# Every 512-column product of a float32r kernel issued as two of 256 columns

## The chip, the cores and the metric

The kernel runs on one core of a Trainium2 chip. The metric is the device time of one execution in microseconds (us). The kernel before takes 1372.56 us, the median of three runs.

## The reference

The program runs two model blocks over 256 tokens with 1024 features in float32. The first has two layers, each a root-mean-square norm, a mixer and a residual sum: an S5 state-space mixer, then block attention with eight heads. The second has two layers of feed-forward, hybrid mixer (a pooling branch and an HGRN2 branch), feed-forward, and a final norm. Nearly all of the arithmetic is products of the tokens with weight matrices. Cut to those:

```python
proj = h @ w_in                                   # S5: 1024 x 2048; attention: 1024 x 4096
y = y * jax.nn.sigmoid(y @ w_glu + b_glu)         # 1024 x 1024
out = y @ w_out                                   # 1024 x 1024, four times in all
def swiglu(x, w_gate, w_up, w_down):              # 1024 x 2816 twice, 2816 x 1024; four times
    return (jax.nn.silu(x @ w_gate) * (x @ w_up)) @ w_down
z = h @ w_in                                      # hybrid mixer: 1024 x 4608, twice
merged = g[:, :, 0] * (pool_out @ w_pool_proj) + g[:, :, 1] * (hgrn_out @ w_hgrn_proj)
return merged @ w_out
```

## The kernel before, in words

**Products in three parts.** A float32 product is made from three float32r products. Each operand is split in two float32r tiles, high and low: weights into WH and WL, tokens into RH and RL (R2H and R2L for a second set, HHI and HLO for the hidden rows of a feed-forward). `mm3` (line 414) issues high × high, high × low and low × high into the same place in PSUM. Each `matmul` brings its own load of the stationary operand, so TensorE's page row counts as many weight loads (PEld) as products (PE). In the profile's names, `P<-RH,WH` is a product that moves RH past stationary WH into PSUM bank P; the products of every helper stand under line 412.

**Two orientations.** Where the result is wanted with features on the partitions, the weights are stationary (128 columns) and the 256 tokens move: `linear` (425), `gate_up_columns` (806), `last_gate` (735), `pool_product` (896). These products have 256 moving columns and write half of a 512-column PSUM bank. Where tokens are wanted on the partitions, 128 tokens are stationary and 512 weight columns move, which fill a whole bank: `out_rows` (454, the four output projections; 32 threes each), `value_rows` (641, 16 threes in each of two mixers), `rows` (664, queries and keys 64 threes, values 32), `gate_up` (786, the first 256 hidden features of each of four feed-forwards, 16 threes each), `gate_rows` (910, 16 in each mixer) and `down` (835, 8 threes for each of 11 blocks of hidden features in four feed-forwards).

**Staging.** The weights come in 222 units of 1 MB through a ring of five slots. SyncE issues a unit's transfer into RAW when the unit that used the slot before is done (`unit_used`, raised by TensorE behind its last product with it). ScalarE copies it into WH (line 1005, `hi_split`), VectorE subtracts to get WL (line 1435, `lo_split`), and TensorE waits for `lo_split`. Each engine's order is written out by hand and the engines meet by semaphores alone.

**Order around the change.** A feed-forward (`ffn`, 848) has eleven blocks of 256 hidden features. The first is made by `gate_up` and turned by transposes; from the second on, `gate_up_columns` issues 96 products of 256 columns, followed by `down` of the block before with 24 products of 512. The last two blocks of `gate_up_columns` stand together, then the remaining 66 and six products of `down` end the block. At its end the residual sum, the norm on VectorE and ScalarE, the transposes (`turn_norm`, 439) and the split of the normed tokens into RH and RL (line 1447) lead into the next block; part of that is laid between products. In the mixers and in attention, short groups of other products (128 columns for the levels, scores and transposes) stand between groups of 24 to 240 long ones.

**The accumulation flag.** A product with `start` set clears the bank's marks of what was written, and a later product without it overwrites where nothing is marked and adds where something is. The kernel relies on this already where two halves of a bank are built in turn: in the first gate unit (line 632) only the first half's product has `start`.

Of the kernel before, what the change touches and what calls it, by code (L numbers as in the profile page):

```python
# [7 lines left out]
KT = DM // 128  # L8
# [96 lines left out]
def build(nc, A, out):  # L105
# [4 lines left out]
    with ctx:  # L110
        def sb(name, shape, dt=f32, c=ctx):
            return c.enter_context(nc.sbuf_tensor(name, shape, dt))


        c = ExitStack()
        RAW = sb("RAW", [128, NW, 2048], c=c)
        c.close()
        c = ExitStack()
# [5 lines left out]
        c = ExitStack()  # L124
# [16 lines left out]
        c = ExitStack()  # L141
        TMPD = sb("TMPD", [128, 2048], c=c)
        c.close()
        c = ExitStack()
# [4 lines left out]
        c = ExitStack()  # L149
# [3 lines left out]
        c = ExitStack()  # L153
# [15 lines left out]
        c = ExitStack()  # L169
# [5 lines left out]
        c = ExitStack()  # L175
# [9 lines left out]
        c = ExitStack()  # L185
# [12 lines left out]
        RH = sb("RH", [128, KT, T], f32r, c=outer)  # L198
        RL = sb("RL", [128, KT, T], f32r, c=outer)
# [3 lines left out]
        c = ExitStack()  # L203
# [20 lines left out]
        c = ExitStack()  # L224
        SG = sb("SG", [128, 2, T], c=c)
        HF = sb("HF", [128, 2, T], c=c)
        HHI = sb("HHI", [128, 3, 2, T], f32r, c=c)
        HLO = sb("HLO", [128, 3, 2, T], f32r, c=c)
        c.close()
        c = ExitStack()  # L230
# [17 lines left out]
        P = [PP[i // 2][:, (i % 2) * 512:(i % 2) * 512 + 512] for i in range(8)]  # L248
# [4 lines left out]
        def tok(a):  # L253
            return slice(a * 128, a * 128 + 128)
# [138 lines left out]
        def _(eng):  # L393
# [20 lines left out]
            def mm3(o, lh, ll, rh, rl, start, stop):  # L414

                mm(o, lh, rh, start=start, stop=False, skip_group_check=True)
                mm(o, lh, rl, start=False, stop=False, skip_group_check=True)
                return mm(o, ll, rh, start=False, stop=stop, skip_group_check=True)

            def weights(u, kt):  # L420

                wh = WH[:, slot_of(u), :].rearrange("p (k c) -> p k c", k=kt)
                return wh, WL[:, slot_of(u), :].rearrange("p (k c) -> p k c", k=kt)
# [30 lines left out]
            def out_rows(u0, i, xh, xl, ready="r_lo", between=None):  # L454


                for n in range(2):
                    for kh, a in ((0, 0), (0, 1), (1, 0), (1, 1)) if n == 0 else ((0, 0), (1, 0), (0, 1), (1, 1)):
                        if kh == 0:
                            free(2 * a + n)  # L460
                        eng.wait_ge(sem["lo_split"], parts_of(u0 + 2 * n + kh))
                        wh, wl = weights(u0 + 2 * n + kh, 4)
                        for k in range(4):
                            kk = 4 * kh + k
                            if n == 0 and a == 0 and k % 2 == 0:
                                eng.wait_ge(sem[ready], pe.next(ready))
                            last = mm3(P[2 * a + n][:, :], xh[:, kk, tok(a)], xl[:, kk, tok(a)],
                                       wh[:, k, :], wl[:, k, :], kk == 0, kk == KT - 1)
                            if n == 1 and a == 1 and kk == 5:
                                turn_norm(i, 0)  # L470
                        if a:
                            last.then_inc(sem["unit_used"], 1)
                        elif kh:
                            last.then_inc(sem["acc_done"], 1)
                        if kh:
                            holds(2 * a + n, "resid")
                        if between is not None and n == 0 and a == 0 and kh == 0:
                            between()
# [27 lines left out]
            for cb in range(1, 4):  # L506
# [6 lines left out]
                for ri in range(2):  # L513
                    for m in range(KT):
                        v = CX[:, ri, m, :]
                        last = nc.tensor.transpose(P[4 + ri * 2 + m // 4][:, (m % 4) * 128:(m % 4) * 128 + 128], v, IDENT)
# [106 lines left out]
            wh, wl = weights(U_GLU, KT)  # L623
# [17 lines left out]
            def value_rows(u0, i, banks):  # L641

                for n in range(len(banks)):
                    for a in range(2):
                        free(banks[n][a])
                        for kh in range(2):
                            u = u0 + 2 * n + kh
                            eng.wait_ge(sem["lo_split"], parts_of(u))
                            wh, wl = weights(u, 4)
                            if n == 0:  # L650
                                eng.wait_ge(sem["xn_lo"], 4 * i - 4 + 2 * a + kh + 1)
                            for k in range(4):
                                kk = 4 * kh + k
                                last = mm3(P[banks[n][a]][:, :], RH[:, kk, tok(a)], RL[:, kk, tok(a)],
                                           wh[:, k, :], wl[:, k, :], kk == 0, kk == KT - 1)
                                if n == 0 and a == 0 and kk == 5:
                                    turn_norm(i, 1)
                            if a:
                                last.then_inc(sem["unit_used"], 1)
                        if not a:  # L660
                            last.then_inc(sem["rows_done"], 1)
                        holds(banks[n][a], "bank_read_a")

            def rows(u, a, bank, part, read):


                if not part:
                    free(bank)
                eng.wait_ge(sem["lo_split"], parts_of(u + part))
                if u == U_QK:  # L670
                    eng.wait_ge(sem["xn_lo"], 4 * N_ATTN - 4 + 2 * a + part + 1)
                wh, wl = weights(u + part, 4)
                for k in range(4):
                    kk = 4 * part + k
                    last = mm3(P[bank][:, :], RH[:, kk, tok(a)], RL[:, kk, tok(a)], wh[:, k, :], wl[:, k, :], kk == 0, kk == KT - 1)
                    if u == U_QK and not a and kk == 5:
                        turn_norm(N_ATTN, 1)
                if a:
                    last.then_inc(sem["unit_used"], 1)
                elif part:  # L680
                    last.then_inc(sem["rows_done"], 1)
                if part:
                    holds(bank, read)
# [102 lines left out]
            def gate_up(u, a, j, i, mid=None):  # L786

                free(4 + a)
                for kh in range(2):
                    eng.wait_ge(sem["lo_split"], parts_of(u + kh))  # L790
                    if j == 0:
                        eng.wait_ge(sem["xn_lo"], 4 * i - 4 + 2 * a + kh + 1)
                    wh, wl = weights(u + kh, 4)
                    for k in range(4):
                        kk = 4 * kh + k
                        last = mm3(P[4 + a][:, :], RH[:, kk, tok(a)], RL[:, kk, tok(a)], wh[:, k, :], wl[:, k, :],
                                   kk == 0, kk == KT - 1)
                        if mid is not None and kk == 5:
                            mid()
                    if a:  # L800
                        last.then_inc(sem["unit_used"], 1)
                if not a:
                    last.then_inc(sem["gu_done"], 1)
                holds(4 + a, "h_made")
# [30 lines left out]
            def down(f, u, j, a, n):  # L835

                eng.wait_ge(sem["lo_split"], parts_of(u))
                eng.wait_ge(sem["h_lo"], 22 * f + 2 * j + (2 if j else a + 1))
                if j == 0:
                    free(2 * a + n)  # L840
                wh, wl = weights(u, 2)
                for k in range(2):
                    last = mm3(P[2 * a + n][:, :], HHI[:, j % 3, k, tok(a)], HLO[:, j % 3, k, tok(a)],
                               wh[:, k, n * 512:n * 512 + 512], wl[:, k, n * 512:n * 512 + 512],
                               j == 0 and k == 0, j == NF - 1 and k == 1)
                return last
# [63 lines left out]
            def gate_rows(u, a):  # L910


                free(a)
                for kh in range(2):
                    if not a:
                        eng.wait_ge(sem["lo_split"], parts_of(u + kh))
                    wh, wl = weights(u + kh, 4)
                    for k in range(4):
                        kk = 4 * kh + k
                        last = mm3(P[a][:, :], RH[:, kk, tok(a)], RL[:, kk, tok(a)], wh[:, k, :], wl[:, k, :], kk == 0, kk == KT - 1)  # L920
                    if a:
                        last.then_inc(sem["unit_used"], 1)
                if not a:
                    last.then_inc(sem["rows_done"], 1)
                holds(a, "bank_read_v")
# [1263 lines left out]
```

## Time and profile before

| what | value |
|---|---|
| median of three runs | 1372.56 us |
| the three runs | 1370.96, 1372.56, 1375.68 us |
| span of the profiled execution, first to last instruction | 1370.1 us |
| TensorE busy, products | 1346.6 us, 9502 products |
| VectorE busy | 868.0 us |
| ScalarE busy | 715.9 us |
| mean granted TensorE clock | 0.999 |
| weights and inputs read | 240.17 MB, 176 GB/s |

The profiled execution's own time is given as its span; the median of the runs is 2.5 us above it. "Busy" for TensorE is the union of overlapping durations: the end of a product is modelled, and a product starts well before the one ahead of it has ended. The distance between two products is read from their starts in the timeline, not from a duration. In the chain that ended last, a piece is a stretch of time on one engine, with the count of instructions in it.

### The profile page before, as it was taken

The numbers are of one execution on the slowest core, as the hardware profiler recorded it, in microseconds if no ns is written. First come the engines' busy times: TensorE is split into PE (matmuls) and PEld (weight loads), VectorE is DVE, ScalarE is ACT, GpSimd is POOL, SyncE is SP. The second block draws the span as 40 slices with busy tenths as digits, with TensorE's granted clock in tenths as the row PEclk, the third lists the DMA queues.
The fourth block names the chain that finished last, engine by engine and source line by source line (L and its number), as shares of the span: only waits on it lengthen the run. The fifth ranks groups of instructions, "written<-read, shape, count | busy, mean of one in ns | idle before, by whom it ended". The sixth has DMA issues, their size and how long they took to land.

```text
span 1370.1 us, 22005 instructions
## 1 busy us (share of the span) xinstructions
PE 1346.6 (98%) x9502; PEld 1244.3 (91%) x9502; DVE 868.0 (63%) x1012; ACT 715.9 (52%) x954; POOL 56.4 (4%) x68
## 2 busy tenths in 40 slices
PE   7998999999999999999999999999999999999998
PEld 6998879889999989998999998999989999899997
DVE  6999676766445567767655547544566857655553
ACT  5998566664444453375544445444454345544443
POOL 1003000000000004000000000000000400000000
PEclk9999999999999999999999999999999999999999
DMA  9106556455656465355555565665556436655552
GB/s 278 53 32 209 180 173 199 140 186 179 201 197 194 167 217 165 120 186 189 195 185 185 192 208 172 201 200 196 201 173 212 152 107 211 198 186 185 185 185 92
DMA packets 180387, 242.63 MB, mean 177 GB/s; under 512 B 7546, under 2 KB 144004, under 8 KB 180292
## 3 DMA queue, kind: packets, MB, share of 16 engines
q1 hardware_dynamic: 178260, 234.92, 52.4%
q0 software_dynamic: 1744, 6.10, 1.6%
q8 instruction: 75, 1.23, 0.4%
q10 hardware_dynamic: 288, 0.22, 0.1%
q14 instruction: 20, 0.16, 0.0%
HBM read 240.17 MB, written 1.05 MB: 176 GB/s over the span
## 4 chain that ended last, share of the span: by engine, by line
PE 96%; ACT 1%; DVE 1%; DMA 1%; issue 0%; DVEq 0%; ACTq 0%; POOLq 0%
PE P L412 94%; PE P L447 1%; DMA G<-in_norm_g 1%; ACT BT L1132 1%; DVE WL L1435 0%; DVE RL L1447 0%; PE P L690 0%; DVE X L1457 0%; ACT YG L1160 0%; PE P L720 0%; ACT Y L1021 0%; DVE YS L1471 0%; ACT RH L1031 0%; ACT WH L1005 0%; PE P L831 0%
## 5 line engine op out<-in xcount | busy, mean ns | idle before, releaser
L1435 DVE TENSOR_TENSOR WL<-RAW,WH 128x2048 fp32r<-128x2048 f32 (+1 forms) x211 | 480.6, 2285 | 304.6 <-ACT WH L1005 303.7
L412 PE MATMUL P<-RH,WH 128*128 128x256 f32 x1856 | 515.9, 278 | 4.0 <-DVE RL L1447 2.7
L412 PE MATMUL P<-RL,WH 128*128 128x256 f32 x1856 | 513.1, 276 | 0.0
L412 PE MATMUL P<-RH,WL 128*128 128x256 f32 x1856 | 513.0, 276 | 0.0
L1005 ACT ACTIVATE WH<-RAW 128x2048 fp32r<-128x2048 f32 x214 | 406.6, 1903 | 189.6 <-DMA RAW<-in_ffn_w_up 78.6
L412 PEld LDWEIGHTS P<-RH,WH 128*128 128x128 f32 x1856 | 348.7, 188 | 5.9 <-DVE RL L1447 2.3
L412 PEld LDWEIGHTS P<-RL,WH 128*128 128x128 f32 x1856 | 348.7, 188 | 1.5
L412 PEld LDWEIGHTS P<-RH,WL 128*128 128x128 f32 x1856 | 348.4, 188 | 0.0
L412 PE MATMUL P<-WH,HLO 128*128 128x512 f32 x352 | 138.7, 394 | 0.0
L412 PE MATMUL P<-WL,HHI 128*128 128x512 f32 x352 | 138.0, 392 | 0.0
L412 PE MATMUL P<-WH,HHI 128*128 128x512 f32 x352 | 136.9, 389 | 0.0
L1316 ACT ACTIVATE SG<-P 128x256 f32<-128x256 f32 x88 | 33.8, 384 | 177.6 <-PE P L412 177.5
L412 PE MATMUL P<-WH,RH 128*128 128x512 f32 x288 | 116.0, 403 | 1.7 <-DVE RL L1447 1.7
L412 PE MATMUL P<-WH,RL 128*128 128x512 f32 x288 | 113.4, 394 | 0.0
L412 PE MATMUL P<-WL,RH 128*128 128x512 f32 x288 | 112.7, 391 | 0.0
L412 PEld LDWEIGHTS P<-WL,HHI 128*128 128x128 f32 x352 | 66.1, 188 | 13.8
L412 PEld LDWEIGHTS P<-WH,HLO 128*128 128x128 f32 x352 | 66.2, 188 | 13.1
L412 PEld LDWEIGHTS P<-WH,HHI 128*128 128x128 f32 x352 | 66.1, 188 | 13.2
L412 PEld LDWEIGHTS P<-WH,RH 128*128 128x128 f32 x288 | 54.2, 188 | 14.1 <-issue 3.0
L412 PEld LDWEIGHTS P<-WH,RL 128*128 128x128 f32 x288 | 54.1, 188 | 11.9
L412 PEld LDWEIGHTS P<-WL,RH 128*128 128x128 f32 x288 | 54.2, 188 | 10.9
L1915 DVE TENSOR_TENSOR HF<-P,SG 128x256 f32<-128x256 f32 x88 | 37.0, 422 | 42.5 <-ACT SG L1316 41.9
(304 smaller groups left out, 1429.5 us busy)
## 6 DMA issues: line engine op xcount, KB each, us to landing
RAW<-in_ffn_w_gate SPq DMA_DIRECT2D x88, 512.0 KB, 4.2
RAW<-in_ffn_w_up SPq DMA_DIRECT2D x88, 512.0 KB, 5.3
RAW<-in_ffn_w_down SPq DMA_DIRECT2D x44, 1024.0 KB, 4.9
RAW<-in_w_in SPq DMA_DIRECT2D x36, 1024.0 KB, 5.1
RAW<-in_attn_w_in SPq DMA_DIRECT2D x16, 1024.0 KB, 5.4
RAW<-in_ssm_w_in SPq DMA_DIRECT2D x8, 1024.0 KB, 9.3
RAW<-in_w_out SPq DMA_DIRECT2D x8, 1024.0 KB, 5.1
RAW<-in_ssm_w_glu SPq DMA_DIRECT2D x4, 1024.0 KB, 6.6
```

Of the source, the lines that this page charges most:

```text
L412: return nc.tensor.matmul(*a, **k)
L447: last = nc.tensor.transpose(P[6 + n][:, k * 128:k * 128 + 128], y[:, a, c:c + 128], IDENT)
L1005: fn(WH[:, s, 0:width], RAW[:, s, 0:width], ACT.Copy).then_inc(sem["hi_split"], 1)
L1132: fn(BT[:, ri, j0:j0 + 4, :], P[4 + g % 4].rearrange("p (j s) -> p j s", j=4), ACT.Copy).then_inc(sem["bt_there"], 1)
L1316: fn(SG[:, a, :], P[4 + a][:, 0:T], ACT.Silu).then_inc(act.raised("gate_done"), 1)
L1435: V.tensor_tensor(WL[:, s, 0:width], RAW[:, s, 0:width], WH[:, s, 0:width].bitcast(f32), SUB).then_inc(sem["lo_split"], 1)
L1915: V.tensor_tensor(HF[:, a, :], P[4 + a][:, T:2 * T], SG[:, a, :], MUL).then_inc(dve.raised("h_made"), 1)
```

## The change

A helper `mm3w` issues what one `mm3` on 512 columns did as two `mm3` on 256 columns each: the three products for the first half of the bank, then the three for the second half. The stationary operands are the same in both halves and are loaded again. Only the first half's first product keeps `start`, since it clears the marks of the whole bank. All six places with 512 moving columns call it.

```diff
+            def mm3w(o, lh, ll, rh, rl, start, stop):
+
+
+                for i in range(2):
+                    c = slice(i * 256, i * 256 + 256)
+                    last = mm3(o[:, c], lh, ll, rh[:, c], rl[:, c], start and i == 0, stop)
+                return last
+
@@ out_rows
-                            last = mm3(P[2 * a + n][:, :], xh[:, kk, tok(a)], xl[:, kk, tok(a)],
+                            last = mm3w(P[2 * a + n][:, :], xh[:, kk, tok(a)], xl[:, kk, tok(a)],
                                        wh[:, k, :], wl[:, k, :], kk == 0, kk == KT - 1)
@@ down
-                    last = mm3(P[2 * a + n][:, :], HHI[:, j % 3, k, tok(a)], HLO[:, j % 3, k, tok(a)],
+                    last = mm3w(P[2 * a + n][:, :], HHI[:, j % 3, k, tok(a)], HLO[:, j % 3, k, tok(a)],
                                wh[:, k, n * 512:n * 512 + 512], wl[:, k, n * 512:n * 512 + 512],
                                j == 0 and k == 0, j == NF - 1 and k == 1)
...
```

The calls in `value_rows`, `rows`, `gate_up` and `gate_rows` change in the same way, `mm3` to `mm3w` and nothing else.

## Rows read from the trace of the kernel before

In a group of a timeline or of the chain the columns are the start in us, the length in us, the engine, the line, the operation, and the number of instructions merged into the row. In a group of the costliest groups they are the form, the count, busy us, mean ns of one, and idle us before it.

**Rows 1.** The page: busy time of the engines; granted clock by slice

```profile
PE 1346.6 (98%) x9502; PEld 1244.3 (91%) x9502; DVE 868.0 (63%) x1012; ACT 715.9 (52%) x954; POOL 56.4 (4%) x68
...
PEclk9999999999999999999999999999999999999999
```

**Rows 2.** Chain that ended last, 640 to 860 us: start us, length us, what

```profile
662.98 166.07 PE P L412 x1200
```

**Rows 3.** The costliest groups, TensorE: products with 512 and with 256 moving columns

```profile
L412 PE MATMUL P<-RH,WH 128*128 128x256 f32 x1856 | 515.9, 278 | 4.0 <-DVE RL L1447 2.7
...
L412 PE MATMUL P<-WH,HHI 128*128 128x512 f32 x352 | 136.9, 389 | 0.0
...
L412 PE MATMUL P<-WH,RH 128*128 128x512 f32 x288 | 116.0, 403 | 1.7 <-DVE RL L1447 1.7
```

**Rows 4.** The same groups listed for TensorE alone

```profile
L412 PE MATMUL P<-XN,RAW 128*128 128x256 f32 x256 | 57.2, 381 | 0.2 <-ACT XN L1073 0.2
...
L412 PE MATMUL P<-WH,R2H 128*128 128x512 f32 x64 | 25.7, 401 | 0.0
```

**Rows 5.** Timeline of TensorE, 626 to 646 us: start us, length us, operation

```profile
625.78 0.39 PE L412 MATMUL P<-WL,RH 128*128 128x512 f32 x1
...
645.92 0.39 PE L412 MATMUL P<-WH,RL 128*128 128x512 f32 x1
```

**Rows 6.** Timeline of TensorE, 612 to 625 us

```profile
611.73 0.28 PE L412 MATMUL P<-R2L,WH 128*128 128x256 f32 x1
...
625.44 0.28 PE L412 MATMUL P<-R2H,WL 128*128 128x256 f32 x1
```

**Rows 7.** Timeline of TensorE, 1140 to 1158 us

```profile
1139.73 0.28 PE L412 MATMUL P<-R2H,WH 128*128 128x256 f32 x1
...
1157.87 0.28 PE L412 MATMUL P<-R2L,WH 128*128 128x256 f32 x1
```

**Rows 8.** Timeline of TensorE, 1160 to 1179 us

```profile
1159.52 0.40 PE L412 MATMUL P<-WH,RH 128*128 128x512 f32 x1
...
1178.88 0.40 PE L412 MATMUL P<-WH,RL 128*128 128x512 f32 x1
```

**Rows 9.** Timeline of TensorE, 130 to 168 us

```profile
130.24 0.36 PE L412 MATMUL P<-RH,WH 128*128 128x256 f32 x1 [1.30 <-DVE WL L1435]
...
147.75 0.40 PE L412 MATMUL P<-WH,R2L 128*128 128x512 f32 x1
...
167.82 0.40 PE L412 MATMUL P<-WL,R2H 128*128 128x512 f32 x1
```

**Rows 10.** Timeline of TensorE, 709 to 711 us

```profile
709.98 0.28 PE L412 MATMUL P<-RH,WH 128*128 128x256 f32 x1
...
710.91 0.28 PE L412 MATMUL P<-RH,WL 128*128 128x256 f32 x1
```

**Rows 11.** Busy by stretch, all engines, granted clock, DMA share

```profile
626.00:646.00 20.00, 20.00 (x89) 16.41 (x88) 16.05 (x17) 12.15 (x14) 0.00 (x0) 1.00 0.51 158
672.00:677.00 5.00, 5.00 (x24) 4.09 (x23) 1.44 (x4) 2.60 (x4) 0.00 (x0) 1.00 0.94 342
612.00:625.00 13.00, 13.00 (x118) 13.00 (x117) 8.48 (x10) 5.12 (x4) 0.00 (x0) 1.00 0.66 222
```

**Rows 12.** The page, DMA queues: packets, MB, share of 16 engines

```profile
q8 instruction: 75, 1.23, 0.4%
```

**Rows 13.** Timeline of TensorE, plain products in the opening stage

```profile
22.71 1.67 PE L412 MATMUL P<-XN,RAW 128*128 128x256 f32 x7
...
51.89 0.60 PE L531 MATMUL P<-CE,BIM 128*128 128x128 f32 x4
...
52.76 0.60 PE L531 MATMUL P<-CE,BIM 128*128 128x128 f32 x4
...
58.73 1.50 PE L412 MATMUL P<-X,BT 128*128 128x64 f32 x12
```

**Rows 14.** What TensorE waited for: us in total, times, longest us

```profile
PE P L412 <- DVE RL L1447: 4.4, 5, 2.1
```

More of the change, by code:

```diff
@@ L653, in value_rows @@
                                 kk = 4 * kh + k
-                                last = mm3(P[banks[n][a]][:, :], RH[:, kk, tok(a)], RL[:, kk, tok(a)],
+                                last = mm3w(P[banks[n][a]][:, :], RH[:, kk, tok(a)], RL[:, kk, tok(a)],
                                            wh[:, k, :], wl[:, k, :], kk == 0, kk == KT - 1)
@@ L674, in rows @@
                     kk = 4 * part + k
-                    last = mm3(P[bank][:, :], RH[:, kk, tok(a)], RL[:, kk, tok(a)], wh[:, k, :], wl[:, k, :], kk == 0, kk == KT - 1)
+                    last = mm3w(P[bank][:, :], RH[:, kk, tok(a)], RL[:, kk, tok(a)], wh[:, k, :], wl[:, k, :], kk == 0, kk == KT - 1)
                     if u == U_QK and not a and kk == 5:
@@ L795, in gate_up @@
                         kk = 4 * kh + k
-                        last = mm3(P[4 + a][:, :], RH[:, kk, tok(a)], RL[:, kk, tok(a)], wh[:, k, :], wl[:, k, :],
+                        last = mm3w(P[4 + a][:, :], RH[:, kk, tok(a)], RL[:, kk, tok(a)], wh[:, k, :], wl[:, k, :],
                                    kk == 0, kk == KT - 1)
@@ L919, in gate_rows @@
                         kk = 4 * kh + k
-                        last = mm3(P[a][:, :], RH[:, kk, tok(a)], RL[:, kk, tok(a)], wh[:, k, :], wl[:, k, :], kk == 0, kk == KT - 1)
+                        last = mm3w(P[a][:, :], RH[:, kk, tok(a)], RL[:, kk, tok(a)], wh[:, k, :], wl[:, k, :], kk == 0, kk == KT - 1)
                     if a:
```

## The prediction

> **What bounds the kernel now.** The first thing to read is the page. TensorE is busy 98% of the span, VectorE 63%, ScalarE 52%, and the granted clock stands at nine tenths or more in every slice [rows 1]; in the stretches read below it is 1.00, the upper of its two levels, 2.4 GHz [rows 11]. A busy share can mislead, so the chain that ended last comes next: from 662.98 us it stays on TensorE's products for 166.07 us, 1200 of them without a break [rows 2]. The longest kind of wait in front of TensorE's products, for the low part of the tokens, is 4.4 us in total over five times [rows 14]. So the time is the number of products times their distance from each other, and nearly every nanosecond of a product's distance is a nanosecond of the kernel.
>
> The page's durations are not those distances. A product with 256 moving columns shows 278 ns and one with 512 shows 389 to 403 ns [rows 3], and by these the split would look ruinous (2 × 278 against 389). But products overlap; only the distance from start to start counts, and the timeline gives it. From 625.78 to 645.92 us there are 88 steps between 512-column products: 20.14 / 88 = **228.9 ns** [rows 5]. From 611.73 to 625.44 us, 121 steps between 256-column products: 13.71 / 121 = **113.3 ns** [rows 6]. Two pieces of 256 cost 226.6 ns, 2.3 ns less than one of 512. A second pace exists. From 1139.73 to 1157.87 us, 154 steps of 256 columns take 18.14 us, 117.8 ns each [rows 7]; from 1159.52 to 1178.88 us, 83 steps of 512 take 19.36 us, 233.3 ns each [rows 8]. The stretch from 147.75 to 167.82 us has it too: 86 steps, 233.4 ns [rows 9]. I call these the fast and the slow pace. The slow one adds about 4.5 ns to a product, whatever its width, and it isn't the clock.
>
> **How many products change.** The groups with 512 columns count 352 for each of three pairs of HHI and HLO, 288 for RH and RL [rows 3], 64 for R2H and R2L [rows 4]: 3 × (352 + 288 + 64) = 2112. Counting the code gives the same 704 threes: 4 × 32 in out_rows, 32 in value_rows, 96 in rows, 64 in gate_up, 32 in gate_rows, 352 in down. So 2112 products and as many weight loads are added to 9502 of each.
>
> **Part one, fast pace.** The two slow stretches hold 90 products each with 512 columns (32 threes of out_rows, less the last two, which stand behind the transposes of the norm), so 1932 of the 2112 run fast. 1932 × (226.6 − 228.9) ns = −4.4 us. This takes the 256-column pace from products whose stationary side is weights and whose moving side is tokens; in the change the sides are swapped, but shapes, types, the order high, low, high and the half bank written are the same, so I take 113.3 unaltered.
>
> **Part two, slow pace.** There two pieces cost 2 × 117.8 = 235.6 against 233.3: 180 × 2.3 ns = +0.4 us, if those stretches stay slow.
>
> **Part three, the joints.** When 256 columns follow 512, the first steps are longer: eight steps from 709.98 to 710.91 us take 0.93 us where 113.3 ns each would be 0.91 [rows 10]. There are 32 such joints in the four feed-forward blocks and two in the mixers. The bounds are nothing and about 0.02 us each, −0.7 us in all; I take −0.6, since afterwards there is one form throughout. Sum: −4.4 + 0.4 − 0.6 = **−4.6 us**.
>
> **What I cost at nothing.** The added weight loads: today each 256-column product already has a load of its own and loads run in parallel, 117 of them beside 118 products in 13 us [rows 11]. The nearest row for how close loads can stand is the plain products with 64 columns: twelve end 1.50 us after the first began, and with 0.27 us for the length of the last (four transposes take 0.60 us, of which three steps are 0.33) eleven steps are 1.23 us, 112 ns each [rows 13]. That floor lies only 1 ns under 113.3, so 256 is about the smallest piece that still covers its load. Fetching the instructions: 75 packets of instructions, 1.23 MB, bring the present program [rows 12]; the new products raise it by some 20%, and a stretch of 1200 products shows no pause [rows 2]. Transfers: 512-column steps number 24 in 5 us with the DMA engines at 0.94 and 89 in 20 us with them at 0.51 [rows 11], so DMA load doesn't set the pace. The waits in front of the norms follow TensorE's own last product and move with it. Other engines gain nothing to do; VectorE would have to work 0.3% faster and has 37% to spare.
>
> The sum is made against a profile whose span is 1370.1 us, which would become 1365.5. The median of the three runs is 2.5 us above that span, so for the median 1372.56 − 4.6 = **1368.0 us**. About 0.3%, 4.1 us, is what a measurement of this kernel can tell from no change, so the forecast lies just over that line.
>
> **A rule against it.** Plain products show a fixed cost: seven with 256 columns end 1.67 us after the first start, so with 381 ns for the length of one [rows 4] a step is (1.67 − 0.38) / 6 = 215 ns; eight transposes take 52.76 − 51.89 = 0.87 us, 108.8 ns each [rows 13]. Two of the small kind cost 217.5 ns, 2.5 more than one large: if that held here, 2112 × 2.5 ns = +5.3 us, and it is part of the first rival below. The Trainium skill, TensorE: Matmul & The Clock Gate, section Back-to-back issue gap, says the same of every product: the columns over 2.4 GHz and 2.5 ns on top. By it 512 columns would take 215.8 ns and two of 256 218.3, which an estimate from that page turns into +5.3 us too. [...]
>
> **The rivals.**
>
> *A cost per instruction (slower).* Beyond twice the 256-column step, a 512-column product pays 2.3 ns. If that is the price of moving weights against stationary tokens, or of switching them, rather than of the width, each half pays it again: 2 × (113.3 + 2.3) = 231.2 ns, +2.3 × 2112 = +4.9 us, 1377.4 us; by the plain products' 2.5 ns it is 1377.9 us. For it: no row shows 256-column products with weights moving, and the plain products carry a cost per instruction. Against: the 113.3 ns are the same for three different pairs of operands. It decides from 1.2 ns per half upward. Chance 0.12. (The rule of the page named above would give this too.)
>
> *The slow pace spreads (slower or nothing).* The slow stretches begin behind a wait and transposes or behind a wait alone (1.30 us at 130.24 [rows 9]) and then persist. More products are more to lose. The 1200 products of one feed-forward block [rows 2] become about 1460; a block that runs slow costs 1460 × 4.5 ns = 6.6 us, which leaves 1374.6 us. The gain is gone with some 1000 products more in the slow pace. Against: all four blocks run fast now. Chance 0.15.
>
> *The slow pace goes away.* The 192 products with 256 and 90 with 512 columns in each slow stretch get back to the fast one: 2 × (192 + 180) × 4.5 ns = −3.3 us more, 1364.7 us. For it: what starts it is a matter of the instant. Chance 0.13.
>
> *The gain is lost in waits.* TensorE arrives sooner and waits longer, for tokens or a weight block; 1372 us. Against: the idle above. Chance 0.06.
>
> **How the numbers follow.** The forecast has the remaining 0.54, with a range of its own from 1366 to 1370 (joints, and a pace read to ±0.1 ns per piece, ±0.4 us, and the scatter of the three runs). Some 0.33 of it lies beyond the 0.3% line, with the vanished slow pace 0.46 for faster. Within 0.3%: 0.21 of the forecast, the lost gain, and the slow pace over a few hundred products up to one block's worth (0.09), together 0.36. Slower: the surcharge and the rest of the slow pace, 0.18. The range is 1364.0 to 1378.0: the low end takes in the vanished slow pace, the high end the cost per instruction and one block in the slow pace.
>
> **What would show it.** In the profile after, TensorE has 11614 products and no form with 512 columns; the stretches of out_rows and of down show steps near 113.3 ns; a down of 24 products, 24 × 228.9 ns = 5.49 us, becomes 48 in 5.44. Steps of 115.6 there would prove the surcharge; steps of 118 the slow pace, and the mean duration of the 256-column groups, 278 ns now [rows 3], would rise. The waits in front of TensorE should stay at their few us, and VectorE and ScalarE keep their busy times. The forecast is wrong if the swapped operands have a pace of their own, which no row of the kernel before shows.

## The result, and the profile after

The changed kernel takes **1384.79 us**, the median of five runs (1383.26 to 1386.84), against 1372.56 us before: a ratio of 1.0089, 95% interval 1.0076 to 1.0102. It is 12.2 us slower where 4.6 us faster was forecast, and it lies above the range given. The page of the profiled execution, whose span is 1381.5 us, has these lines for [rows 1] and [rows 12]:

```profile
PE 1358.4 (98%) x11614; PEld 1346.9 (98%) x11614; DVE 868.6 (63%) x1012; ACT 715.8 (52%) x954; POOL 54.3 (4%) x68
...
PEclk9999999999999999999999999999999999999999
...
q8 instruction: 92, 1.51, 0.5%
```

There are 2112 products more and as many loads, the clock is as before, VectorE and ScalarE are busy for as long as before, and the instructions come in 92 packets where there were 75. The waits of TensorE didn't grow either; the row for [rows 14] (us in total, times, longest) is

```profile
PE P L412 <- DVE RL L1455: 4.7, 5, 2.2
```

So the 11.4 us between the two spans are neither waits nor clock. In the chain that ended last, the piece that answers to [rows 2] is the second feed-forward block (start us, length us):

```profile
668.23 167.93 PE P L412 x1458
```

1458 products take 167.93 us where 1200 took 166.07. TensorE's groups of long products, for [rows 3] (count, then busy us and mean ns of one, then idle us before them):

```profile
L412 PE MATMUL P<-RH,WH 128*128 128x256 f32 x1856 | 518.3, 279 | 4.4 <-DVE RL L1455 3.0 <-DVE WL L1443 1.4
L412 PE MATMUL P<-RH,WL 128*128 128x256 f32 x1856 | 515.6, 278 | 0.0
L412 PE MATMUL P<-RL,WH 128*128 128x256 f32 x1856 | 515.6, 278 | 0.0
L412 PE MATMUL P<-WH,HHI 128*128 128x256 f32 x704 | 195.9, 278 | 0.0
...
L412 PE MATMUL P<-WH,RH 128*128 128x256 f32 x576 | 163.7, 284 | 1.7 <-DVE RL L1455 1.7
```

No form with 512 columns is left. The mean length of the untouched 256-column products (RH and RL moving) is 279 or 278 ns where it was 278 or 276, and that small shift leads to the cause. In the timeline, first a stretch of halves with moving weights in the output rows of the first mixer, 178 steps from the first row to the last:

```profile
630.80 0.28 PE L412 MATMUL P<-WL,RH 128*128 128x256 f32 x1
...
650.98 0.28 PE L412 MATMUL P<-WH,RL 128*128 128x256 f32 x1
```

20.18 / 178 = 113.4 ns: the pace forecast for a half exists. Next, two streams that the change does not touch, `gate_up_columns` of two neighbouring blocks of hidden features in one feed-forward block, 83 steps and 81 steps:

```profile
683.80 0.28 PE L412 MATMUL P<-RH,WH 128*128 128x256 f32 x1
...
693.57 0.28 PE L412 MATMUL P<-RH,WL 128*128 128x256 f32 x1
```

```profile
700.83 0.28 PE L412 MATMUL P<-RL,WH 128*128 128x256 f32 x1
...
710.01 0.28 PE L412 MATMUL P<-RL,WH 128*128 128x256 f32 x1
```

9.77 / 83 = 117.7 ns and 9.18 / 81 = 113.3 ns. The same code, with the same operands, runs slow once and fast once. This is the second pace of [rows 7]. The stretches of busy time (length of the stretch, then busy us and count of PE, PEld, DVE, ACT and POOL, granted clock, DMA share, GB/s) show it in order, `down`, columns, `down`, columns:

```profile
677.20:682.20 5.00, 5.00 (x47) 5.00 (x46) 1.50 (x4) 2.53 (x4) 0.00 (x0) 1.00 0.95 330
683.00:693.00 10.00, 10.00 (x88) 10.00 (x87) 6.88 (x4) 4.11 (x3) 0.00 (x0) 1.00 0.36 116
694.00:699.00 5.00, 5.00 (x45) 5.00 (x45) 1.18 (x3) 2.60 (x4) 0.00 (x0) 1.00 0.93 334
700.00:710.00 10.00, 10.00 (x90) 10.00 (x90) 6.44 (x4) 4.23 (x3) 0.00 (x0) 1.00 0.39 108
```

In 5 us, 47 products and then 45; in 10 us, 88 and then 90; the clock is 1.00 in all four, and the DMA share is the same in the fast `down` and in the slow one (0.95, 0.93). The change of pace falls on the first product with moving tokens behind a `down`:

```profile
682.04 0.28 PE L412 MATMUL P<-WH,HHI 128*128 128x256 f32 x1
682.15 0.28 PE L412 MATMUL P<-WL,HHI 128*128 128x256 f32 x1
682.27 0.28 PE L412 MATMUL P<-WH,HLO 128*128 128x256 f32 x1
682.38 0.28 PE L412 MATMUL P<-RH,WH 128*128 128x256 f32 x1
682.50 0.28 PE L412 MATMUL P<-RL,WH 128*128 128x256 f32 x1
682.62 0.28 PE L412 MATMUL P<-RH,WL 128*128 128x256 f32 x1
682.74 0.28 PE L412 MATMUL P<-RH,WH 128*128 128x256 f32 x1
```

The three steps up to 682.38 take 0.34 us together, the three behind it 0.36. In the feed-forward blocks this goes on regularly: a fast `down`, a slow stream of columns, a slow `down`, a fast stream, and again. In attention and the mixers, halves with moving weights run slow almost wherever they stand behind transposes (between 203 and 208 us the mean length of two of the three forms is 279 ns):

```profile
L412 PE MATMUL P<-WL,RH 128*128 128x256 f32 x15 | 4.2, 279 | 0.0
L412 PE MATMUL P<-WH,RL 128*128 128x256 f32 x14 | 3.9, 279 | 0.0
```

To see how much each kind of product pays, I summed in every trace the distance from a product's start to the next one's start, by kind of product. "Slow" counts the 256-column products whose step lies between 116.4 and 125 ns. The step of the very last product, which belongs to `down`, is taken up to the end of the span (6.0 us in every row).

```
                      span    tokens move (slow)   down (slow)     other rows (slow)  rest
before               1370.1   686.98 us   (610)    250.46 us       248.02 us          174.76 us
after                1381.5   692.93     (1925)    252.19 (928)    251.75 (1706)      174.78
e1_down_only         1381.8   695.66     (2549)    253.41 (1194)   247.85             174.59
e2_all_but_down      1372.4   685.95      (385)    250.44          251.75 (1708)      174.42
e3_pairs             1382.3   693.51     (2117)    251.62 (793)    252.06 (1707)      174.86
e4_anchor            1371.1   687.89      (579)    248.44 (18)     249.97 (1048)      174.78
e5_joint_only        1379.7   694.19     (2264)    252.40 (96)     247.90             175.18
e6_down_anchor       1369.2   687.87      (686)    248.62 (58)     247.74             174.99
e8_kick              1377.1   691.74      (433)    248.19 (31)     252.00 (1686)      175.16
e9_kick_linear       1367.8   686.63      (447)    249.02 (143)    247.35             174.93
e10_best             1369.7   687.36      (528)    248.63 (58)     247.77 (181)       176.06
```

"Tokens move" are the 5976 untouched 256-column products, "other rows" all with moving weights outside `down`. Of the 11.4 us, **6.0 us lie in products that the change doesn't touch**, 1.7 in `down` and 3.7 in the other rows. Each row of the table is one execution: that of e1_down_only lies 2.8 us above the median of its four runs, and the ratios below are of all runs of a kernel, not of this one.

The same steps, read from the starts in the traces, show what happens at a joint. In the four feed-forward blocks a `down` is followed by a stream of columns without a pause at 32 places (joints), and a stream of columns by a `down` at 36. The pace is kept at all 36 in every kernel but e7_quarters, whose `down` has neither pace. At the 32 it is this:

```
pace of down -> pace of the columns behind it      fast->fast  fast->slow  slow->fast
last products of down whole:  before, e2, e4           32 each      0           0
                              e6, e9, e10           31, 29, 31      0        1, 3, 1
last products of down halves: after, e1, e3, e5           0      16 each     16 each
halves, then two of 128 tokens: e8                       32           0           0
```

In the 64 streams that stay slow, none of the first eight steps is longer than 120 ns. In all 288 streams that go on fast in these eleven kernels, one of them is 121 ns or longer, and the fast steps follow it. In the kernel before the stream at 677.17 us begins with steps of 117, 117, 117, 123 and 118 ns and goes on at 113; in the changed kernel that at 682.38 us begins with 119, 119, 117 and 119 and stays there. So the fast streams of the kernel before begin slow too, and leave the slow pace with one longer step. Whether that step is the cause or only the mark of the change, no run shows.

### The profile page after: what moved, and what is told of

It is laid out like the page before. It is cut to its first block, busy times and chain, and to the rows that moved or that the text cites. A ratio compares the mean times of both kernels' runs of the same rounds, so it can differ in the third digit from the quotient of the medians.

```text
span 1381.5 us, 26229 instructions
## 1 busy us (share of the span) xinstructions
PE 1358.4 (98%) x11614; PEld 1346.9 (98%) x11614; DVE 868.6 (63%) x1012; ACT 715.8 (52%) x954; POOL 54.3 (4%) x68
## 4 chain that ended last, share of the span: by engine, by line
PE 89%; DVE 9%; issue 1%; DMA 1%; ACT 0%; DVEq 0%; ACTq 0%; POOLq 0%
PE P L412 87%; PE P L455 1%; DVE QQ L1768 1%; DVE WL L1443 1%; DMA G<-in_norm_g 1%; DVE YG L1747 0%; DVE RL L1455 0%; DVE WB L1758 0%; DVE QQ L1772 0%; DVE TMPC L1719 0%; DVE TMPC L1716 0%; DVE QQ L1759 0%; DVE X L1732 0%; DVE TMPD L1685 0%; DVE TMPD L1717 0%
## 5 line engine op out<-in xcount | busy, mean ns | idle before, releaser
L412 PE MATMUL P<-WH,HHI 128*128 128x256 f32 x704 | 195.9, 278 | 0.0
L412 PE MATMUL P<-WH,HLO 128*128 128x256 f32 x704 | 195.3, 277 | 0.0
L412 PE MATMUL P<-WL,HHI 128*128 128x256 f32 x704 | 195.2, 277 | 0.0
L412 PE MATMUL P<-WH,RH 128*128 128x256 f32 x576 | 163.7, 284 | 1.7 <-DVE RL L1455 1.7
L412 PE MATMUL P<-WL,RH 128*128 128x256 f32 x576 | 160.6, 279 | 0.0
L412 PE MATMUL P<-WH,RL 128*128 128x256 f32 x576 | 160.5, 279 | 0.0
L412 PEld LDWEIGHTS P<-WH,HHI 128*128 128x128 f32 x704 | 132.2, 188 | 0.0
L412 PEld LDWEIGHTS P<-WH,HLO 128*128 128x128 f32 x704 | 132.2, 188 | 0.0
L412 PEld LDWEIGHTS P<-WL,HHI 128*128 128x128 f32 x704 | 132.1, 188 | 0.0
L412 PEld LDWEIGHTS P<-WH,RH 128*128 128x128 f32 x576 | 108.2, 188 | 2.4 <-issue 2.2
```

Of the source, the lines that this page charges most:

```text
L412: return nc.tensor.matmul(*a, **k)
```

## The experiments

Theory S: the pace is a state of the stream, set at the joints between kinds of product, and every product behind a joint pays it. Theory P: the loss is a price that each half with moving weights has by itself. The ratio given is to the kernel before, run on the same chip in the same series.

**e1_down_only.** `mm3w` only in `down`; in the other five places `mm3` again (shown against the changed kernel, arguments left out).

```diff
@@ out_rows, value_rows, rows, gate_up, gate_rows
-    last = mm3w(
+    last = mm3(
```

> Only the products of down are split (1056 become 2112); the other 1056 with 512 columns stay whole. Theory S (the pace is a state that the joints between streams set, and every product of the stream behind a joint pays it): the feed-forward blocks run as in the changed kernel, so down costs +1.7 us and the untouched 256-column products between them about +5.5 us: some +7 us against the kernel before. Theory P (a price of its own on each half with moving weights): only the +1.7 us of down, and the untouched 256-column products keep their 113.4 ns.

Measured: 1380.85 us against 1372.59, ratio 1.0060 (1.0043 to 1.0077). The untouched products pay 8.7 us in the profile, `down` 3.0. P, which left the untouched ones alone, falls. The total is 8.3 us where S expected some 7.

**e2_all_but_down.** The other half of the edit: `mm3` in `down`, `mm3w` elsewhere.

> The other half of the change: everything but down is split. Both theories expect about +3.7 us from the split products themselves. Theory S: inside the feed-forward blocks, where each stream of 256-column products again follows 512-column ones, the pace goes back to fast everywhere, so the total is near +4 us. Theory P expects the same there; if the total were +8 us or more, the state would be carried across blocks.

Measured: 1375.98 us, ratio 1.0032 (1.0020 to 1.0044). The other rows pay their 3.7 us and the untouched products nothing (1.0 us less than before). With whole products in `down` the state isn't carried through the feed-forward blocks.

**e3_pairs.** The order of the halves.

```diff
-                for i in range(2):
-                    c = slice(i * 256, i * 256 + 256)
-                    last = mm3(o[:, c], lh, ll, rh[:, c], rl[:, c], start and i == 0, stop)
+                for p, (l, r) in enumerate(((lh, rh), (lh, rl), (ll, rh))):
+                    for i in range(2):
+                        c = slice(i * 256, i * 256 + 256)
+                        last = mm(o[:, c], l, r[:, c], start=start and p == 0 and i == 0, stop=stop and p == 2, skip_group_check=True)
```

> The same 4224 halves in another order: high x high for both halves, then high x low for both, then low x high for both, so that the loaded weights change at every second product. If the slow pace comes from how loads and products fall against each other (theory S), another order gives another share of slow products, in the split streams above all, and the sum may fall anywhere from -5 us (all fast) to +15 us (all slow). Theory P: order does not matter, +12 us as in the changed kernel.

Measured: 1384.11 us, ratio 1.0086 (1.0072 to 1.0100), as the changed kernel. The order of the loads inside a product's halves isn't what sets the pace. P expected this too, so the run doesn't tell the theories apart; the streams alternate here as they do in the changed kernel.

**e4_anchor.** As the changed kernel, with some whole products among the halves.

```diff
@@ mm3w
+                if whole:
+                    return mm3(o, lh, ll, rh, rl, start, stop)
@@ down
-                               j == 0 and k == 0, j == NF - 1 and k == 1)
+                               j == 0 and k == 0, j == NF - 1 and k == 1, a == n == k == 1)
@@ out_rows, value_rows, rows, gate_up, gate_rows
-                               kk == 0, kk == KT - 1)
+                               kk == 0, kk == KT - 1, kk % 6 == 0)
```

> As the changed kernel, but the three products behind each break stay whole: kk 0 and 6 in the row products, and the last three of each down. 1452 or so of 2112 stay split. Theory S: before, a stream behind a 512-column product was always fast, so nearly all is fast: about -3 us from the split products, none lost in the untouched ones, 1369 to 1371 us at a median before of 1372.6. Theory P: the loss shrinks only with the number of halves, to about +8 us.

Measured: 1371.46 us, ratio 0.9991 (0.9982 to 1.0001). The loss is gone (the interval holds 1), though 1716 of the 2112 products are still split (924 in `down`, 792 elsewhere; the expectation's 1452 was a miscount). In `down` nearly all is fast (18 slow). In the other rows whole products behind the transposes did not help: 1048 halves are slow. What worked, in `down`, is the whole products ahead of the joint.

**e5_joint_only and e6_down_anchor.** The two complements inside `down`, everything else whole.

```diff
@@ down, e5_joint_only
-                    last = mm3(P[2 * a + n][:, :], HHI[:, j % 3, k, tok(a)], HLO[:, j % 3, k, tok(a)],
+                    split = a == n == k == 1
+                    last = (mm3w if split else mm3)(P[2 * a + n][:, :], HHI[:, j % 3, k, tok(a)], HLO[:, j % 3, k, tok(a)],
@@ down, e6_down_anchor
-                    last = mm3(P[2 * a + n][:, :], HHI[:, j % 3, k, tok(a)], HLO[:, j % 3, k, tok(a)],
+                    split = not (a == n == k == 1)
+                    last = (mm3w if split else mm3)(P[2 * a + n][:, :], HHI[:, j % 3, k, tok(a)], HLO[:, j % 3, k, tok(a)],
```

> From the kernel before, only the last three products of each down are split (a = n = k = 1: 132 products become 264); everything else is whole. Theory S: whole products bring the stream to the joint in the same phase each time, and six halves followed by tokens that move turn it to the slow pace, so nearly every 96-product stream behind a down is slow: 32 x 96 x 4.5 ns = up to +13.8 us, or half of that (+7) if the slow pace survives the whole products of down and every second joint turns it back. Theory P (the loss lies in the split products): 132 x 2.3 ns = 0.3 us, no change to be seen.

> The counterpart: down is split except for the last three products of each call with a = n = 1 (k = 1); everything outside down is whole. 924 of the 1056 products are split. Theory S: every joint is as in the kernel before, so the feed-forward blocks are fast throughout: 924 x -2.3 ns = -2.1 us (1370.5 at a median before of 1372.6), plus or minus what the other slow stretches do by chance (about 3 us if both go). Theory P: as the run with down alone, about +6 us less an eighth.

Measured: e5_joint_only, which splits 132 products, 1381.75 us, ratio **1.0061** (1.0045 to 1.0077); e6_down_anchor, which splits the other 924, 1370.09 us against 1372.17, ratio **0.9981** (0.9973 to 0.9990). The groups of TensorE tell which pace a stream of columns has. In e5_joint_only, first the stream between 330 and 340 us, then the next one, between 347 and 356 us:

```profile
L412 PE MATMUL P<-RL,WH 128*128 128x256 f32 x29 | 8.1, 281 | 0.0
```

```profile
L412 PE MATMUL P<-RL,WH 128*128 128x256 f32 x27 | 7.5, 276 | 0.0
```

and in e6_down_anchor between 330 and 340 us, as in every stream behind a `down`:

```profile
L412 PE MATMUL P<-RL,WH 128*128 128x256 f32 x31 | 8.6, 276 | 0.0
```

281 ns is the slow pace, 276 the fast. The second feed-forward block of e6_down_anchor is, in its chain,

```profile
663.86 165.57 PE P L412 x1428
```

0.50 us shorter than in [rows 2]. That an eighth of the split products makes a kernel 0.6% slower, while the other seven eighths make it 0.2% faster, leaves nothing of P. In e6_down_anchor's profile `down` takes 1.8 us less than before, near the 924 × 2.3 ns = 2.1 us that halves at the fast pace save. In e5_joint_only 16 of the 32 streams behind a `down` are slow, every second one, which is the second of the two cases that were expected: the whole products of `down` carry the slow pace on (21 steps of 233.5 ns behind a slow stream, 229.0 behind a fast one), and the next joint turns it back.

**e7_quarters.** Four pieces of 128 columns in `down`, everything else whole.

```diff
-                for i in range(2):
-                    c = slice(i * 256, i * 256 + 256)
+                for i in range(4):
+                    c = slice(i * 128, i * 128 + 128)
```

> Down alone, each 512-column product as four of 128 columns. If the load of the stationary operand sets a floor for small pieces (about 112 ns by the plain 64-column products), four cost at least 448 ns against 229: 1056 x 219 = +231 us, to which +0 to +20 us of slow pace in other products may come. If a piece of 128 columns could run at half of 113.3 ns, the time would stay near 1373.

Measured: 1599.19 us, one run, against 1372.17: +227 us. From the timeline:

```profile
348.92 0.28 PE L412 MATMUL P<-WH,HLO 128*128 128x128 f32 x1
...
351.93 0.27 PE L412 MATMUL P<-WH,HLO 128*128 128x128 f32 x1
```

There are 27 steps from the first row to the last: 3.01 / 27 = 111.5 ns. A piece of 128 columns costs nearly as much as one of 256 (113.3 ns), and the plain products of 64 columns take 112 ns [rows 13]: a float32r product of 128 columns with a load of its own isn't faster than that. That it is the load which sets this floor is likely but not shown, since no run issues such a product without one. A half lies less than 2 ns above it.

**e8_kick.** The changed kernel; the first product of each `gate_up_columns` pair is issued as two of 128 tokens.

```diff
+                        if kk == e == i == 0:
+                            o = P[4 + i][:, 0:T]
+                            mm(o[:, 0:128], wh[:, 0, cc], RH[:, 0, 0:128], start=True, stop=False, skip_group_check=True)
+                            mm(o[:, 128:256], wh[:, 0, cc], RH[:, 0, 128:256], start=False, stop=False, skip_group_check=True)
...
```

> The changed kernel, and the first product of each gate_up_columns stream is issued as two of 128 tokens (40 products more, each about 112 ns in place of half of 113.3: +2.2 us in themselves). Theory S: the disturbance at the joint is now another one, so the regular change of fast and slow streams in the feed-forward blocks breaks up; the untouched 256-column products (1925 slow ones in the changed kernel) end either mostly fast (total near 1378) or mostly slow (near 1392). Theory P: streams alternate as before, 1387.

Measured: 1378.87 us, one run, span 1377.1. The untouched products at the slow pace fall from 1925 to 433 and those in `down` from 928 to 31, though 40 products were added. This is the first of the two outcomes that S expected. Changing what stands at the joint changes the pace of whole streams behind it.

**e9_kick_linear and e10_best.** To find out whether the streams that start behind a wait or behind transposes can be turned too: e9_kick_linear is e6_down_anchor with the same pair of 128 tokens at the start of three streams; e10_best splits 270 products of `out_rows` behind them as well.

```diff
+                        if kick and h == k == 0:
+                            mm(o[:, 0:128], wh[:, k, cc], xh[:, k, 0:128], start=True, stop=False, skip_group_check=True)
+                            mm(o[:, 128:256], wh[:, k, cc], xh[:, k, 128:256], start=False, stop=False, skip_group_check=True)
...
@@ out_rows, e10_best alone
+                            split = i != N_FFN[0] and not (n == 1 and a == 1 and kk > 5)
```

> The run e6 plus, at the start of the three streams that ran slow now and then after a pause (the second gate unit at about 130 us, and the first product of the two branch projections in each mixer, about 604 and 1136 us), one product issued as two of 128 tokens. In the run e8 each such pair turned the stream behind it to the fast pace. Theory S: these three streams and the rows behind them run fast: some 380 to 560 products x 4.5 ns less 3 x 0.12 us, so -1.5 to -2.2 us against e6, about 1368.5 at a median before of 1372.2. If a stream that starts behind a pause finds its pace otherwise (by the instant of its start), nothing changes against e6 (1370.1) or a stream goes either way. Theory P: no change.

> As e9, and the rows of the state-space output and of the two mixers' output are split too, up to the transposes inside them (3 x 90 = 270 products), since they follow a stream that should be fast. Theory S: 270 x -2.3 ns = -0.6 us more if those streams are fast, 1367.9, a ratio near 0.997; if they come in slow, their halves take 235.6 ns against 233.4 and it is +0.2 us each. Theory P: +1 us against e9.

Measured: e9_kick_linear 1369.78 us against 1371.87, ratio 0.9982 (0.9972 to 0.9993), no better than e6_down_anchor (0.9981); e10_best 1370.95, ratio 0.9995 (0.9986 to 1.0003). In e9_kick_linear's profile all three streams run fast (113.7 or 113.8 ns a step), but in e10_best the second of the three, with the same edit, runs slow (118.1 ns), and the 180 halves behind it run at 117.8. The pair turns a stream that follows another without a pause, and doesn't settle one that starts behind a pause (the slow one began 0.75 us after TensorE had gone idle, its like in e9_kick_linear without idle time): my expectation for these was wrong, and its other case, that a stream goes either way, is what was seen. In e9_kick_linear's profile the opening 78 products of columns run slow in three of the four feed-forward blocks, against one in e6_down_anchor's; what turns those was not tried.

## Why the prediction was wrong

**Right:** that TensorE's steps alone make the time; the number of products; waits, clock, loads in number, instruction fetch, VectorE and ScalarE cost nothing (the rows above). The price of a fast half, 113.4 ns, and of a slow one, 117.8, were both right, and so was the floor for small pieces close under them (111.5 ns by e7_quarters against 112 estimated).

The formula of the Trainium skill weighed there, TensorE: Matmul & The Clock Gate, section Back-to-back issue gap, isn't what happened. By it a half would take 109.2 ns and a whole product 215.8, and no stream of float32r products here runs at either: the steps are 113.3 or 117.8 and 228.9 or 233.4 ns. The section gives the formula for an isolated product and says that in a stream of loads and products the spacing differs from it both ways; the prediction left that out. Plain products of 256 columns don't agree with it either: they take 215 ns [rows 13] where it gives 109.2. What the plain products share with it is only the surcharge of about 2.5 ns for each.

**The step that failed** is part one, "1932 × (226.6 − 228.9) ns", which took the fast pace for all halves of streams that had been fast, and with it the argument against the second rival, "all four blocks run fast now". In whole form these streams were fast because of what stood at their joints, and the change replaced just that. Instead, 2634 of the 4224 halves ran at 117.8 ns. Halves behind transposes run slow nearly everywhere, where whole products had run at their 229; and six halves ahead of a joint turn a fast stream slow, where whole products didn't. In numbers: if all 2112 pairs were fast, −4.9 us, and −0.8 for the 180 products that had been slow; 2634 halves are slow, 2634 × 4.5 ns = +11.9; 1315 more of the untouched products at the slow pace, +5.9. That is +12.1 us, where 11.4 were measured.

**The rivals.** The second, "the slow pace spreads", is what happened, with a chance of 0.15. Its price was drawn too small: I priced one block (+6.6 us) in place of half of every block and the rows outside. I also called what starts the slow pace "a matter of the instant". Behind a pause or transposes that may hold: the streams ahead of the output rows of the two mixers (192 products, the same code) ran fast and then slow in the kernel before, both fast in the changed kernel and both slow in e6_down_anchor, which edits neither. At a joint without a pause it repeats itself at all 32 places of a run, in each of the four kernels with plain halves ahead of the joint. The first rival, a cost per instruction, is refuted by the 178 steps at 113.4 ns. The joints (part three, −0.6 us) were the place where it was decided; I had measured that the first steps behind one are longer, took it for a small cost, and didn't ask what state they leave behind: they are steps at the slow pace, and behind the longer one among them the fast pace begins.

**Open:** what in TensorE holds the two paces, and what at a joint turns them. The runs show when it happens, not the mechanism. The traces narrow it a little: in both paces a load starts some 3 ns after the product ahead of it; the product then starts 110 ns after its load in the fast pace of the changed kernel (701 to 709 us) and 114 or 115 ns after it in the slow one (684 to 693 us). So it is the distance from load to product that grows. That the two steps, of a small piece and of 256 columns, are nearly equal (111.5 and 113.3 ns) makes it plausible that loads and products lock against each other, but whole products of 512 columns have the slow pace too (233.4 ns), at twice that step. Shape alone isn't what turns the pace: in the changed kernel the products on both sides of a joint have 256 columns, and it turns where tokens move behind weights (32 of 32) and never where weights move behind tokens (0 of 36). Why the halves behind transposes run slow (3.7 us of the loss) was located by e2_all_but_down and not explained; with whole products among them (e4_anchor) 1048 of 1584 were still slow.

## What to carry to other kernels

When an engine runs back to back, look at the start-to-start steps stretch by stretch, not at one representative stretch: if the same instruction shows two steps, an edit can move the share of each, in code that it doesn't touch. The first steps behind a change of operands deserve a look of their own. Before an engine-wide change of the issue pattern, try it on one kind of stream and leave whole what stands just ahead of a change of operands; here that turned +0.9% into −0.2% (e6_down_anchor, 1370.09 us, the version that beats both). And don't cut such products, with a load each, below 256 columns: a piece of 128 costs 111.5 ns where one of 256 costs 113.3.

## What the runs showed that was not expected

The products with float32r operands have two stable paces at the same granted clock of 1.00: 113.3 and 117.8 ns for 256 columns, 228.9 and 233.4 for 512. A pace persists through hundreds of products (192 and then 132 in one run of the changed kernel). Two products of 128 tokens in front of a stream of columns brought the fast pace in all 36 streams of e8_kick that went on without transposes; behind a pause or transposes the same pair left one stream of six slow (three in e9_kick_linear, three in e10_best). In the kernel before, a stream of columns behind a `down` begins at the slow pace though it ends fast, and in every trace here only a step of 121 ns or more among the first eight leads out of it.
